# Inverse root of the q and k norm by Ln, Exp and a Newton step, and its mean as two F32R products, in a Trainium2 encoder block

## The reference

```python
def rms_norm(x, g):
    xf = x.astype(jnp.float32)
    y = xf * lax.rsqrt(jnp.mean(xf * xf, axis=-1, keepdims=True) + NORM_EPS)
    return (y * g.astype(jnp.float32)).astype(x.dtype)
...
        z = h @ w_in[l]
        q = z[..., :o1].reshape(B, S, N_Q_HEADS, HEAD_DIM)
        k = z[..., o1:o2].reshape(B, S, N_KV_HEADS, HEAD_DIM)
...
        q = apply_rope(rms_norm(q, q_norm_g[l]), cos, sin)
        k = apply_rope(rms_norm(k, k_norm_g[l]), cos, sin)
        y_attn = block_attention(q, k, v) @ w_attn_branch[l]
```

## Time and profile before

| | us |
|---|---|
| median of 3 runs | 3081.8 |
| lowest and highest | 3079.35, 3087.96 |
| the profiled execution, its own time | 3081.74 |
| its span | 3079.9 |
| TensorE busy | 3002.9 (98%) |
| VectorE busy | 2370.0 (77%) |
| ScalarE busy | 1451.9 (47%) |
| GpSimd busy | 574.8 (19%) |

### The profile page before, as it was taken

One profiled execution on the slowest core, in us unless ns is written; L12 is line 12 of the kernel. 1 busy time (PEld: TensorE's weight loads), 2 busy tenths in 40 slices (PEclk: granted clock), 3 DMA queues, 4 the chain that ended last, 5 costly groups with the idle time before them and its releaser, 6 DMA issues.

```text
span 3079.9 us, 35419 instructions
## 1 busy us (share of the span) xinstructions
PE 3002.9 (98%) x13417; PEld 2418.7 (79%) x13417; DVE 2370.0 (77%) x2302; ACT 1451.9 (47%) x1856; POOL 574.8 (19%) x513
## 2 busy tenths in 40 slices
PE   5999999999999999999999999999999999999998
PEld 4777777777788888877888778888888888888887
DVE  6679687776499999997566789999564899996453
ACT  5433111111799999983333444444343444444433
POOL 0011522532000000000000244443120444440000
PEclk9999999999999999999999999999999999999999
DMA  8643332223721111148666332222664222226663
GB/s 338 216 150 135 130 112 80 86 100 124 228 52 38 35 39 35 39 128 248 188 218 218 132 110 82 82 83 82 218 215 166 93 82 83 82 83 218 215 211 126
DMA packets 159322, 408.11 MB, mean 133 GB/s; under 512 B 17992, under 2 KB 38472, under 8 KB 154664
## 3 DMA queue, kind: packets, MB, share of 16 engines
q1 hardware_dynamic: 141472, 352.88, 35.2%
q0 software_dynamic: 10192, 36.18, 3.1%
q10 hardware_dynamic: 7488, 16.78, 1.4%
HBM read 296.51 MB, written 104.02 MB: 130 GB/s over the span
## 4 chain that ended last, share of the span: by engine, by line
PE 66%; DVE 4%; ACT 1%; DMA 1%; issue 1%; POOL 0%; SPq 0%; ACTq 0%; DVEq 0%; POOLq 0%
PE second_ps_a L91 8%; PE second_ps_a L93 8%; PE second_ps_a L92 8%; PE second_ps_b L91 8%; PE second_ps_b L93 8%; PE second_ps_b L92 8%; PE att_ps_o L1597 7%; PE att_ps_s L1582 4%; PE att_ps_s L1583 4%; PE att_ps_r L1610 2%; DMA merge_x<-in_w_out 1%; PE att_ps_r L1615 0%; PE second_ps_b L1841 0%; DVE att_prob_lo L1519 0%; DVE ffn_x L2925 0%
## 5 line engine op out<-in xcount | busy, mean ns | idle before, releaser
L1519 DVE TENSOR_TENSOR att_prob_lo<-att_prob,att_prob_hi 128x1024 fp32r<-128x1024 f32 x256 | 309.9, 1221 | 24.1 <-ACT att_prob_hi L1479 22.9
L91 PE MATMUL second_ps_a<-up_in_hi,up_wu_hi 128*128 128x512 f32 x728 | 284.0, 390 | 5.1 <-DVE up_wu_lo L2375 3.1
L2911 DVE TENSOR_TENSOR ffn_wd_lo<-ffn_wd_st,ffn_wd_hi 128x1024 fp32r<-128x1024 f32 x110 | 130.6, 1224 | 201.9 <-ACT ffn_wd_hi L2734 201.9
L93 PE MATMUL second_ps_a<-up_in_hi,up_wu_lo 128*128 128x512 f32 x728 | 283.3, 389 | 0.0
L92 PE MATMUL second_ps_a<-up_in_lo,up_wu_hi 128*128 128x512 f32 x728 | 283.3, 389 | 0.0
L1479 ACT ACTIVATE att_prob_hi<-att_prob 128x1024 fp32r<-128x1024 f32 x256 | 272.2, 1064 | 0.0
L1473 ACT ACTIVATE att_prob<-att_ps_s 128x1024 f32<-128x1024 f32 x256 | 262.4, 1026 | 9.9 <-PE att_ps_s L1583 9.9
L2734 ACT ACTIVATE ffn_wd_hi<-ffn_wd_st 128x1024 fp32r<-128x1024 f32 x110 | 110.8, 1052 | 243.1 <-PE second_ps_a L93 132.1
L917 ACT ACTIVATE proj_out<-proj_ps,proj_bg 128x512 f32<-128x512 f32 x64 | 44.1, 689 | 378.2 <-PE proj_ps L93 365.5
L1597 PE MATMUL att_ps_o<-att_prob_hi,heads_kv 128*128 128x512 f32 x512 | 200.1, 391 | 1.8 <-DVE att_prob_lo L1519 1.7
L1597 PE MATMUL att_ps_o<-att_prob_lo,heads_kv 128*128 128x512 f32 x512 | 199.4, 389 | 0.0
(11 more groups left out here) (352 smaller groups left out, 8180.5 us busy)
## 6 DMA issues: line engine op xcount, KB each, us to landing
ffn_wd_st<-in_w_dn SPq DMA_DIRECT2D x110, 512.0 KB, 4.9
up_w_st<-in_w_up SPq DMA_DIRECT2D x44, 512.0 KB, 3.6
ffn_g_raw<-scratch_g SPq DMA_DIRECT2D x88, 192.0 KB, 4.2
scratch_gates<-proj_out SPq DMA_DIRECT2D x64, 256.0 KB, 2.0
early_w_st<-in_w_branch SPq DMA_DIRECT2D x32, 512.0 KB, 7.0
merge_gate<-scratch_gates SPq DMA_DIRECT2D x64, 256.0 KB, 3.7
up_w_st<-in_w_up SPq DMA_DIRECT2D x44, 256.0 KB, 4.1
up_w_a<-in_w_up SPq DMA_DIRECT2D x44, 256.0 KB, 4.3
```

What stands on the lines that cost most here:

```text
L91: pe.matmul(out, w_hi, x_hi, start=first, stop=False)
L93: return pe.matmul(out, w_lo, x_hi, start=False, stop=last)
L1519: dve.tensor_tensor(prob_lo[:, s % LAG, :], prob[:, s % RING, :], prob_hi[:, s % LAG, :], ALU.subtract)\
L2911: dve.tensor_tensor(wd_lo[split_at(m)][:], wd_st[staged_at(m)][:], wd_hi[split_at(m)][:], ALU.subtract).then_inc(s_dlo, 1)
```

## The change

The mean of squares goes over to two F32R products. ScalarE writes the square as before, then a rounded copy of it (`sq_hi`); VectorE writes the rest, with the norm's epsilon added (`squares_lo`); TensorE adds up two products with the averaging matrix, which is copied once to F32R (`mrow`). The inverse root is made without a root and a reciprocal: ScalarE takes Ln, then Exp with a factor of -0.5, which gives an approximate inverse root r, and r squared (`inverse_root`); VectorE makes one Newton step of it, r (1.5 - 0.5 m r r), in two operations (`newton`), and multiplies the rotated block by it (`normed`). The order of the loops on ScalarE and VectorE is written anew. `s_zg` counts the copy with the gain alone, and a semaphore `s_sq` counts the square and the rounded copy. Everything before and behind the 20 blocks stays.

```diff
-                def root(c, n):
-                    act.wait_ge(s_ms, 4 * c + n + 1)
-                    if c or n >= 2:
-                        act.wait_ge(s_rot, 4 * c + n - 1)
-                    act.activation(std[:, n % 2, :], ps_ms[:, n % 2, :], ACT.Sqrt, bias=eps[:, 0:1]).then_inc(s_std, 1)
+                def inverse_root(i):
+                    at = std[:, i % 2, :]
+                    act.wait_ge(s_ms, i + 1)
+                    act.activation(at, ps_ms[:, i % 2, :], ACT.Ln).then_inc(s_std, 1)
+                    act.wait_ge(s_std, 3 * i + 1)
+                    act.activation(at, at, ACT.Exp, scale=-0.5).then_inc(s_std, 1)
+                    act.wait_ge(s_std, 3 * i + 2)
+                    act.activation(sq[:, i % 2, :], at, ACT.Square).then_inc(s_std, 1)
...
-                        act.wait_ge(s_mm, 4 * c + n + 1)
-                        if c or n >= 2:
-                            act.wait_ge(s_rot, 4 * c + n - 1)
-                        act.activation(zg[:, n % 2, :], ps[n], ACT.Copy, scale=gains[:, c:c + 1])
-                        act.activation(sq[:, n % 2, :], ps[n], ACT.Square).then_inc(s_zg, 1)
-                        if c or n >= 2:
-                            rotated_hi(4 * c + n - 2)
-                        if n:
-                            root(c, n - 1)
-                    root(c, NB - 1)
+                        i = NB * c + n
+                        act.wait_ge(s_mm, i + 1)
+                        if i >= 2:
+                            act.wait_ge(s_rot, i - 1)
+                        act.activation(zg[:, n % 2, :], ps[n], ACT.Copy, scale=gains[:, c:c + 1]).then_inc(s_zg, 1)
+                        act.activation(sq[:, n % 2, :], ps[n], ACT.Square).then_inc(s_sq, 1)
+                        act.wait_ge(s_sq, 2 * i + 1)
+                        act.activation(sq_hi[:, n % 2, :], sq[:, n % 2, :], ACT.Copy).then_inc(s_sq, 1)
+                        if i:
+                            inverse_root(i - 1)
+                        if i >= 2:
+                            rotated_hi(i - 2)
+                inverse_root(NROPE - 1)
...
+                dve.wait_ge(s_c, 16 * 3)
+                dve.tensor_copy(mrow[:], head_mean).then_inc(s_sqlo, 1)
                 dve.wait_ge(s_rt, 16 * 2)
+
+                def squares_lo(i):
+                    at = sq[:, i % 2, :]
+                    dve.wait_ge(s_sq, 2 * i + 2)
+                    dve.scalar_tensor_tensor(sq_lo[:, i % 2, :], at, EPS, sq_hi[:, i % 2, :], ALU.add, ALU.subtract).then_inc(s_sqlo, 1)
...
+                def newton(i, step):
+                    root, square = std[:, i % 2, :], sq[:, i % 2, :]
+                    if step == 0:
+                        dve.wait_ge(s_std, 3 * i + 3)
+                        dve.scalar_tensor_tensor(square, square, -0.5, ps_ms[:, i % 2, :], ALU.mult, ALU.mult).then_inc(s_nr, 1)
+                    else:
+                        dve.wait_ge(s_nr, 2 * i + 1)
+                        dve.scalar_tensor_tensor(root, square, 1.5, root, ALU.add, ALU.mult).then_inc(s_nr, 1)
+
+                def normed(i):
+                    dve.wait_ge(s_rope, 3 * i + 3)
+                    dve.wait_ge(s_nr, 2 * i + 2)
+                    if i >= NB:
+                        dve.wait_ge(s_st[i % NB], 32 * (i // NB))
+                    dve.tensor_tensor(out[:, i % NB, :], rot[:, i % 2, :], std[:, i % 2, :], ALU.mult).then_inc(s_rot, 1)
+
                 for c in range(NQC + 1):
                     lo_part(c + 1, (c + 1) % 2)
...
-                        dve.reciprocal(sc, sc).then_inc(s_rope, 1)
...
+                    for i in range(NB * c, NB * (c + 1)):
+                        squares_lo(i)
+                        if i:
+                            newton(i - 1, 0)
+                        if i >= 2:
+                            rotated_lo(i - 2)
+                        if i:
+                            newton(i - 1, 1)
+                            normed(i - 1)
+                        rotate(i)
                 lo_part(NQKV, 0)
+                newton(NROPE - 1, 0)
+                rotated_lo(NROPE - 2)
+                newton(NROPE - 1, 1)
+                normed(NROPE - 1)
                 rotated_lo(NROPE - 1)
...
-                    pe.wait_ge(s_zg, 4 * c + n + 1)
+                    pe.wait_ge(s_sqlo, 4 * c + n + 2)
...
-                    pe.matmul(ps_ms[:, n % 2, :], head_mean, sq[:, n % 2, :], start=True, stop=True).then_inc(s_ms, 1)
+                    at = ps_ms[:, n % 2, :]
+                    pe.matmul(at, mrow[:], sq_hi[:, n % 2, :], start=True, stop=False)
+                    pe.matmul(at, mrow[:], sq_lo[:, n % 2, :], start=False, stop=True)\
+                        .then_inc(s_ms, 1)
```

More of the change, by code:

```diff
@@ L647, in proj_phase @@
                             for a in (2, 3) for b in (0, 1))
+        sq_hi, sq_lo = (nc.alloc_sbuf_tensor_at(f"proj_squares_{n}", [P, 2, BLK], F32R, offset=side_at + (a * 4 + b * 2) * BLK * 4)
+                        for n, a, b in (("hi", 3, 0), ("lo", 2, 1)))
         z, eo = (side[:, a, :].rearrange("p (n c) -> p n c", n=N1) for a in range(2))
@@ L658, in proj_phase @@
             r.sem(n) for n in ("w_hi_made", "w_lo_made", "products", "zg_sq", "mean", "root", "rotated", "v_or_gate", "rope"))
+        s_sq, s_sqlo, s_nr = (r.sem(n) for n in ("squares_steps", "squares_lo", "newton_steps"))
         s_sw = [r.sem(f"pairs_swapped{i}") for i in range(2)]
@@ L935, in _, with rotate @@
                 dve.memset(eps[:], EPS).then_inc(s_eps, 1)
+                dve.wait_ge(s_c, 16 * 3)
+                dve.tensor_copy(mrow[:], head_mean).then_inc(s_sqlo, 1)
                 dve.wait_ge(s_rt, 16 * 2)
+                def squares_lo(i):
+                    at = sq[:, i % 2, :]
+                    dve.wait_ge(s_sq, 2 * i + 2)
+                    dve.scalar_tensor_tensor(sq_lo[:, i % 2, :], at, EPS, sq_hi[:, i % 2, :], ALU.add, ALU.subtract).then_inc(s_sqlo, 1)
+                def rotate(i):
+                    cols = slice(i % NB * BLK, (i % NB + 1) * BLK)
+                    zc, rc = zg[:, i % 2, :], rot[:, i % 2, :]
+                    dve.wait_ge(s_sw[i % 2], 32 * (i // 2 + 1))
+                    dve.tensor_tensor(rc, rc, sin[:, cols], ALU.mult).then_inc(s_rope, 1)
+                    dve.tensor_tensor(zc, zc, cos[:, cols], ALU.mult).then_inc(s_rope, 1)
+                    dve.wait_ge(s_rope, 3 * i + 2)
+                    dve.tensor_tensor(rc, rc, zc, ALU.add).then_inc(s_rope, 1)
@@ L1023, in _ @@
                         if c:
-                            pe.wait_ge(s_zg, 4 * (c - 1) + n + 1)
+                            pe.wait_ge(s_sq, 2 * (4 * (c - 1) + n) + 1)
                         if c <= NQC and n >= 2:
```

## The result

The changed kernel takes 3125.0 us (median of 4 runs, 3122.8 to 3128.3) against 3081.1 us before (median of 4 runs as well): slower by 43.9 us, ratio 1.0131 with a 95% interval of 1.0118 to 1.0143. The prediction was 3119 us in a range of 3108 to 3138. The profiled execution took 3126.9 us, its span is 3125.0, 45.1 more than before.

A forecast was written before the change was run, and what follows sets the result against it. VectorE set the pace before, 6.9 us per block; a ScalarE-VectorE loop of 9.0 us would after. 3081.74 us + 36.5 (later first transposition of v) + 0.7 (TensorE's clock) = 3119 us, range 3108 to 3138.

The forecast's parts named there:

- The loop and the loads: In the 20 blocks, each waits for a whole ScalarE-VectorE loop with two table loads, 1.31 us each plus 0.10 lost overlap.
- Rival (a): Each load in the blocks costs double, 2 x 1.28 us more per period: +46, 3165 us; chance 0.07.
- rival (b): Loads overlap VectorE's part, ScalarE's own work bounds the blocks at 7.0 us each: 3084 us, no change; chance 0.04.
- rival (c): Loads in the blocks cost nothing since the set in place serves; period 6.4 us, -8.2: 3073.5 us; chance 0.05.
- rival (d): TensorE stays at 1.2 GHz through the phase, 10.9 us for a block: +121, 3202 us; chance 0.04.
- The size of a period: One trip of the ScalarE-VectorE loop, from one block's L895 to the next: 9.02, taken as 9.0 us.
- A_2: Moment at which ScalarE starts L895, the copy with the gain, of block 2; forecast at 180.1 us.
- A_19: Moment at which ScalarE starts L895 of block 19; forecast 180.1 + 17 x 9.0 = 333.1 us, against 297.58.
- The start: TensorE starts block 2 at about 174.0 in place of 171.7 and ends it at 179.5 us.
- The end: First transposition of v 25.0 us after A_19, at 358.1 against 321.60: +36.5 us; slack of 1.7 us covers the first gate.
- TensorE's savings: Two F32R products for the mean free 20 x 0.37 = 7.4 us on TensorE, hidden in its idle time.
- TensorE's idle time: TensorE needs 5.9 us per block, so it idles 3.1 us in each and is busy some 65%.

The follow-up runs named there:

- run 5: Changed kernel with all 40 loads, but ScalarE makes the previous block's inverse root ahead of the copy with the gain, VectorE follows; 3093.0 us against 3084.6 before.
- run 1: Changed kernel with one table load ahead of the rotation, of the set holding Ln and Exp, none in the blocks; 3079.6 us against 3086.1 before.
- run 2: Changed kernel with one load in each block instead of two, of the set holding both functions; 3099.3 us against 3086.1 before.
- run 9: Changed kernel with VectorE making the first squares' low part ahead of the rotation table wait and the weights' low part; 3127.3 us against 3088.1 before.
- Run 3: Changed kernel with the mean again as one plain float product, inverse root and two loads kept; 3110.2 us against 3086.1 before.
- run 6: The order of run 5 with one load ahead of the rotation and none in it; 3077.6 us against 3084.6 before.
- run 8: Changed kernel's order with the plain float mean and one load ahead of it all; 3079.2 us against 3084.6 before.
- run 4: Kernel before with only the mean changed to two F32R products, root and reciprocal as before; 3106.0 us against 3086.1 before.

## Why the prediction came out as it did

**The loop and the loads: right.** "L895 of block i+1 waits for the multiplication of block i-1": run 5 opens this gate with the loads in place and takes back 34 us; run 1 takes the loads out and leaves the gate, and takes back 46. Both are needed for the loss. The load's own price, 1.31 us and 0.10 for a lost overlap, came out as 1.27 and 1.42 in run 2, and (9.15 - 6.46) / 2 = 1.35 in run 1. Rival (a), a load of double cost, has the gaps of 0.01 to 0.02 us against it; rival (b), ScalarE's own work as the bound, has the two-sided waits, and its 7.0 us came only in run 5; rival (c), loads that cost nothing, has the 40 loads of 1283 ns and run 2; rival (d), the low clock throughout, has the granted clock of 0.89.

The drain of about 1.38 us that the Trainium skill ("ScalarE: Activation LUTs", What ACT_TABLE_LOAD costs) puts beside the load at a switch of set did not show in this loop, by the same gaps. The set with both functions that the Trainium skill names (the same page, Table sets: the hidden batching unit) served for both in run 1, but only once it was loaded by hand.

**The size of a period: 0.18 us short.** I said 9.0, rounded from 9.02; from A_2 to A_19 it is 155.99 / 17 = 9.18, with trips of 9.15 to 9.18 and a single one of 9.42. The operations came as taken up to VectorE's start at 6.38. Behind it the old low part takes 0.60 where I took 0.54 from a row of 630 ns (it is now 684), and the last multiplication starts 0.08 us after the second Newton operation ends, where I took 0.03. In all, the 17 periods are 3.0 us longer than forecast, the largest miss that the runs explain.

**The start: 2 us short.** That TensorE "ends it at 179.5" (block 2) assumed full speed. The clock fell right there. Stretches of the changed kernel:

```profile
174.20:176.50 2.30, 2.26 (x8) 1.83 (x9) 1.60 (x3) 2.27 (x3) 0.00 (x0) 0.73 0.16 61
176.50:179.00 2.50, 2.50 (x8) 1.97 (x7) 1.69 (x4) 1.69 (x3) 0.00 (x0) 0.56 0.00 0
```

TensorE ended block 2 at 181.9, 1.7 us later than at full speed, and ScalarE waited for it. I had priced such a fall at 1.4 us and taken half, but ahead of the last four blocks, where the granted clock in fact was 1.00 (338 to 363 us). The place was wrong, the size about right; run 9, with no fall, got 1.5 us back.

**The end: right.** A_19 + 25.0 was the transposition's time to the hundredth (338.05, 363.05). The slack behind it held as well, though little was left: the first gate ends at 368.53, and the second transposition comes at 368.99, 5.94 us after the first, as before.

**TensorE's savings: right in this kernel.** Its 7.4 us of savings are hidden, as said. Run 3 shows more: the F32R mean costs 16 us here. In run 6 the same part pays in the trace, against run 8: 314.03 to 309.63, where TensorE is the bound in both; the medians (3077.6, 3079.2) are too close to tell.

**TensorE's idle time: wrong, without effect.** I expected it busy "some 65%" of the time and idle 3.1 us in each block. It was busy 123.2 of the 155.99 us between A_2 and A_19, 79%, because in part of them it ran at half speed. Two neighbouring periods, near the two ends of what occurs:

```profile
191.23:200.41 9.18, 8.82 (x39) 6.72 (x37) 5.18 (x9) 7.71 (x11) 1.08 (x2) 1.00 0.43 145
200.41:209.57 9.16, 5.49 (x13) 4.36 (x14) 6.21 (x10) 6.74 (x9) 1.08 (x2) 0.63 0.22 86
```

The granted clock is 1.00 in one and 0.63 in the other, and the periods are equally long: as the prediction had it, a fall inside the loop costs nothing.

**The sum.** The profiled execution took 3126.9 us, 7.9 more than forecast. The periods account for 3.0 of it and the start for 2.0; the 0.7 us for the clock at the end was not needed; and 3.7 came behind the first transposition, where the prediction had nothing. In the traces of all eleven kernels the time from the first transposition to that late table load lies between 2563.5 us (run 6) and 2575.1 us (run 5), 2570.9 in run 1, which has no loads in its blocks. So 3.7 us is within what this stretch varies by, and it says nothing about the change.

## What to carry to other kernels

Look at the built program for table loads before pricing a function by its duration: two functions that share a set can still be built as two loads, and one load by hand can serve all. An engine's idle time is no cover if its work lies in a loop of handovers; walk from an event back to itself, add up, and compare the sum with each engine's own work. Such a loop is often opened by order alone: put what does not depend on the gate ahead of it.

## What the runs showed of the hardware

A load of the set that is already in place takes the same 1.28 us (run 2, 20 loads of 1283 ns).

The prediction's rows had a fall of TensorE's clock after an idle time of 3.28 us. Ahead of block 2 the granted clock fell to half, from 2.4 to 1.2 GHz, after shorter ones: 2.40 us in the changed kernel, 2.12 in run 1, 2.15 in run 4 and 2.99 in run 5. It stayed at 1.00 after 2.12 us in run 2 and 2.27 in run 6. So in this range the length of the idle time alone does not decide. In the changed kernel's loop the granted clock was 0.89 on average, with idle times of 2.9 to 4.0 us in 8 of the 17 periods.
